# Moving the recurrence's sum and what follows it to later slots in a pipelined encoder layer

## The reference

```python
xn = rmsnorm(x, norm_pre_w)
na_q, na_k, na_v, na_z, hg_q, hg_ff, hg_fb, hg_i, hg_z, gate_pre = split(xn @ w_in)
o_a = neighbourhood_attention(na_q, na_k, na_v, rpb) * silu(na_z)       # 16 heads of 64
o_b = scan(hg_q, k_fwd, hg_i, log_f_fwd) + flip(scan(flip(...)))        # 8 heads of 128, both directions
o_b = rmsnorm(o_b, hg_norm_w) * silu(hg_z)                              # per head of 128 channels
g_a, g_b = split(sigmoid(gate_pre + b_gate))
y = g_a * (o_a @ w_branch[:1024]) + g_b * (o_b @ w_branch[1024:])
out = x + rmsnorm(y @ w_out, norm_post_w)
```

## Time and profile before

| | us |
|---|---|
| median of 3 runs | 835.32 |
| lowest, highest | 834.16, 838.45 |
| the profiled execution | 836.1 |
| its span, first to last instruction | 834.4 |
| mean granted clock of PE in it | 0.997 |
| PE busy | 820.7 (98%) |
| DVE busy | 632.1 (76%) |
| ACT busy | 413.7 (50%) |
| POOL busy | 40.2 (5%) |

### The profile page before, as it was taken

How to read it: one execution, slowest core, us unless ns; L and a number is a source line. 1 busy time by engine, 2 the same in 40 slices (tenths; PEclk the granted TensorE clock), 3 DMA queues, 4 the chain that set the end, 5 groups by cost and what they waited for, 6 DMA issues and landing times.

```text
span 834.4 us, 15319 instructions
## 1 busy us (share of the span) xinstructions
PE 820.7 (98%) x5582; PEld 703.8 (84%) x5582; DVE 632.1 (76%) x1053; ACT 413.7 (50%) x706; POOL 40.2 (5%) x48
## 2 busy tenths in 40 slices
PE   9999999999999999999999999999999999999996
PEld 8888788888888888888888888888888888878884
DVE  4777747888888888888888897897785778765443
ACT  5744445445445445445445435535545555544442
POOL 5000100000000000000100000100000000000002
PEclk9999999999999999999999999999999999999998
DMA  9755777676576676566667666666557767675522
GB/s 329 277 178 181 198 190 182 174 196 165 160 196 164 167 195 171 159 181 170 174 179 180 167 168 168 188 166 186 155 160 195 220 188 197 202 275 193 185 104 101
DMA packets 246729, 153.98 MB, mean 185 GB/s; under 512 B 15288, under 2 KB 228368, under 8 KB 246288
## 3 DMA queue, kind: packets, MB, share of 16 engines
q1 hardware_dynamic: 245664, 149.17, 63.0%
q10 hardware_dynamic: 1008, 3.98, 1.3%
HBM read 151.04 MB, written 2.10 MB: 184 GB/s over the span
## 4 chain that ended last, share of the span: by engine, by line
PE 92%; DVE 4%; ACT 1%; issue 1%; POOL 0%; DMA 0%; POOLq 0%; ACTq 0%
PE psum L1174 47%; PE psum L1176 23%; PE psum L1416 3%; PE psum L1418 3%; PE psum L1417 3%; DVE w_lo L711 2%; PE psum L1227 2%; PE psum L1229 2%; PE psum L1228 2%; PE psum L1278 1%; ACT w_hi L448 1%; PE psum L1266 1%; PE psum L1243 1%; PE psum L1313 1%; PE psum L1256 1%
## 5 line engine op out<-in xcount | busy, mean ns | idle before, releaser
L1174 PE MATMUL psum<-act_hl,w_hi 128*128 128x512 f32 x1408 | 501.6, 400 | 1.7 <-DVE hg L732 1.0
L1176 PE MATMUL psum<-act_hl,w_lo 128*128 128x256 f32 x1408 | 394.4, 280 | 0.0
L711 DVE TENSOR_TENSOR w_lo<-raw,w_hi 128x1024 fp32r<-128x1024 f32 x272 | 323.7, 1228 | 81.9 <-ACT w_hi L448 81.6
L1174 PEld LDWEIGHTS psum<-act_hl,w_hi 128*128 128x128 f32 x1408 | 264.3, 188 | 66.3 <-issue 2.3
L448 ACT ACTIVATE w_hi<-raw 128x1024 fp32r<-128x1024 f32 x272 | 273.7, 1053 | 39.5 <-PE psum L1418 25.8
L1176 PEld LDWEIGHTS psum<-act_hl,w_lo 128*128 128x128 f32 x1408 | 265.8, 189 | 0.0
L462 ACT ACTIVATE part<-psum 128x256 f32<-128x256 f32 x88 | 33.7, 383 | 214.8 <-PE psum L1176 214.8
L1174 PE MATMUL psum<-branch_hl,w_hi 128*128 128x512 f32 x256 | 88.9, 394 | 0.0
L1176 PE MATMUL psum<-branch_hl,w_lo 128*128 128x256 f32 x256 | 70.9, 277 | 0.0
L1174 PEld LDWEIGHTS psum<-branch_hl,w_hi 128*128 128x128 f32 x256 | 48.0, 188 | 11.1
L1227 PE MATMUL psum<-w_hi,branch_hl 128*128 128x512 f32 x128 | 50.3, 393 | 1.0 <-DVE w_lo L711 1.0
(11 more groups left out here) (137 smaller groups left out, 686.3 us busy)
## 6 DMA issues: line engine op xcount, KB each, us to landing
raw<-in_w_in SPq DMA_DIRECT2D x103, 1024.0 KB, 5.8
raw<-in_w_branch SPq DMA_DIRECT2D x16, 1024.0 KB, 6.0
raw<-in_w_out SPq DMA_DIRECT2D x16, 1024.0 KB, 5.0
bias_t<-in_na_rel_bias SPq DMA_DIRECT2D x32, 96.0 KB, 5.8
big<-in_x SPq DMA_DIRECT2D x4, 512.0 KB, 8.4
big<-in_x ACTq DMA_DIRECT2D x2, 1024.0 KB, 6.1
out<-big SPq DMA_DIRECT2D x5, 256.0 KB, 2.7
raw<-in_w_in SPq DMA_DIRECT2D x2, 512.0 KB, 6.5
```

Source lines behind the costliest of these rows:

```text
L711: nc.vector.tensor_tensor(w_lo[:, i, :], raw[:, r, 1024 * h:1024 * (h + 1)], w_hi[:, i, :].bitcast(F32), ALU.subtract).then_inc(lo_ready, 1)
L1174: nc.tensor.matmul(sums[h][:, :], w_hi[:, i, w], operand[:, k, :], start=first, stop=False, skip_group_check=True)
L1176: ins = nc.tensor.matmul(sums[h][:, 0:T], w_lo[:, i, w], operand[:, k, 0:T], start=False, stop=last, skip_group_check=True)
```

## The change

The sum moves on PE from slot 6 to slot 9, behind the early near session of the next group. What follows it becomes a third routine, `finish(g - 2, s)`, that runs in the group after that: squares and mean square in slot 0, scaling in slot 1, the turn on PE in slot 2 ahead of the late near session, the output product in slot 2, its rounding and subtraction in slot 3. The tanh of `hz` moves on ACT from slot 0 to slot 4 and the output gate on DVE from slot 8 to slot 5, both still one group behind. DVE's `take_nearest` gets a wait for the sum, which reads the same scores. POOL's loop runs the power of group g - 2 ahead of the mask's add of group g. The tail does the same steps for its two last groups.

POOL:

```diff
             mask_bias(0)
-            with loop(pool, 1, NG) as g:
+            mask_bias(1)
+            with loop(pool, 2, NG) as g:
+                power(g - 2)
                 mask_bias(g)
-                power(g - 1)
+            power(NG - 2)
             power(NG - 1)
```

ACT:

```diff
                 if s == 0:
-                    tanh_half((hth, hz), g - 1, NSLOT_HZ, hz_tanh)
                     act.wait_ge(oa_ready, g)
...
-                if s == 6:
-                    out_square(g - 1)
-                if s == 7:
-                    out_scale(g - 1)
-                if s == 9:
-                    hgrn_hi(g - 1)
+                if s == 4:
+                    wait(act, ob_ready, g - 1)
+                    tanh_half((hth, hz), g - 1, NSLOT_HZ, hz_tanh)
+
+            def finish(g, s):
+
+                if s == 0:
+                    out_square(g)
+                if s == 1:
+                    out_scale(g)
+                if s == 3:
+                    hgrn_hi(g)
```

DVE:

```diff
                 if s == 9:
+                    if not first:
+                        dve.wait_ge(hg_out, g)
                     take_nearest(g)
...
-                if s == 8:
-                    hgrn_out(g - 1)
-                if s == 9:
-                    hgrn_lo(g - 1)
+                if s == 5:
+                    output_gate(g - 1)
+
+            def finish(g, s):
+
+                if s == 0:
+                    mean_square(g)
+                if s == 2:
+                    hgrn_out(g)
+                if s == 3:
+                    hgrn_lo(g)
...
                     split_tile(*place(g0, p, s + 1)[0:2])
+                    if third:
+                        finish(g - 2, s)
                     if not first:
                         previous(g, s)
                     attention(g, s, first)
-                    if s == 6 and not first:
-                        mean_square(g - 1)
```

PE:

```diff
-                if s == 5:
-                    hgrn_sum(g - 1)
-                if s == 7:
-                    turn_out(g - 1)
+            def finish(g, s):
+                if s == 1:
+                    turn_out(g)
...
+                            if third:
+                                finish(g - 2, s - 1)
                             if not first:
                                 previous(g, s - 1)
                             attention(g, s - 1)
+                            if s == IN_SLOTS - 1 and not first:
+                                hgrn_sum(g - 1)
```

More of the change, by code:

```diff
@@ L535, in previous, with group @@
                     nc.scalar.activation(i_now[:, :], at(big, g * 3 + (I_HOME - 3)), ACT.Copy).then_inc(i_ready, 1)
-                if s == 6:
-                    out_square(g - 1)
-                if s == 7:
-                    out_scale(g - 1)
-                if s == 9:
-                    hgrn_hi(g - 1)
-            def group(g0, p, first):
+                if s == 4:
[8 more added lines that the diff above has]
+                    hgrn_hi(g)
+            def group(g0, p, first, third=False):
                 g = g0 + p
@@ L625, in _ @@
                 for p in range(2):
-                    group(g0, p, False)
+                    group(g0, p, False, True)
             for t in range(TAIL):
@@ L631, in _ @@
                 previous(NG, t)
+                finish(NG - 2, t)
+                if t == 6:
+                    out_square(NG - 1)
+                if t == 7:
+                    out_scale(NG - 1)
                 take_part(place(NG, 0, t)[0], t % 2)
@@ L903, in mean_square, with output_gate @@
                 nc.vector.tensor_scalar(hg_ms, hg_ss, 1.0 / P, EPS, ALU.mult, ALU.add).then_inc(ms_ready, 1)
+            def output_gate(g):
+                dve.wait_ge(hz_tanh, g + 1)
+                nc.vector.scalar_tensor_tensor(out=hth, in0=hth, scalar=1.0, in1=hz, op0=ALU.add,
+                                               op1=ALU.mult).then_inc(ob_step, 1)
             def hgrn_out(g):
[L907 to L912, removed]
+                dve.wait_ge(ob_step, g + 1)
                 dve.wait_ge(o_turned, g + 1)
@@ L1384, in _, with tail_between @@
                 for p in range(2):
-                    group(g0, p, False)
+                    group(g0, p, False, True)
+            def tail_between(t):
+                if t == 0:
+                    attention(NG - 1, IN_SLOTS - 1)
+                else:
+                    finish(NG - 2, t - 1)
+                    previous(NG, t - 1)
+                if t == 6:
+                    hgrn_sum(NG - 1)
             for t in range(TAIL):
@@ L1388, in _ @@
                 pe.wait_ge(tile_out, made(NG, t - 2))
-                project(n, r, [ps_proj[t % 2]] * 2, act_hl,
-                        lambda: previous(NG, t - 1) if t else attention(NG - 1, IN_SLOTS - 1))
-            previous(NG, TAIL - 1)
+                project(n, r, [ps_proj[t % 2]] * 2, act_hl, lambda: tail_between(t))
+            turn_out(NG - 1)
             def branch(n, r, j):
```

2 lines of the change are left out of this document (1 added, 1 removed).

## The result

| | kernel before | changed kernel |
|---|---|---|
| median of the runs | 836.0 us (6 runs, 834.16 to 838.45) | 844.06 us (6 runs, 840.66 to 850.14) |
| profiled execution, its span | 836.1, 834.4 | 844.07, 842.3 |
| busy on PE, DVE, POOL | 820.7, 632.1, 40.2 | 822.3, 629.9, 38.9 |

The change makes the kernel slower: ratio 1.0093, with a 95% interval of 1.0072 to 1.0115. The forecast was 842.5. Sign and size came out, but most of the sum did not: of 7.9 us of span only 2.3 lie at the wait on which the forecast put 6.9. The changed kernel's own runs also spread more than those of the kernel before, and their mean granted clock differs: 0.998 in the fastest (840.66), 0.989 in the slowest (850.14), 0.994 to 0.996 in the four between.

The account below looks back on a forecast made before the run. PE, busy 98%, bounds the kernel; its own terms were 0, waits 6.9 us: span 834.4 + 6.9 = 841.3, 843.0 as an execution, 842.2 on the median's footing, stated as 842.5, range 836.5 to 847.5.

Parts of the forecast that it names:

- the wait on which the forecast put 6.9: PE waiting at the late near session for DVE's level 6 products, 0.72 to 1.44 us in each of groups 2 to 7.
- PE's own terms: On PE, moving the sum costs 0; joining the output's turn to another interruption saves 0 to 0.6 us, taken as 0.
- The pace: Half tiles on PE run quick or slow, 0.05 us apart; moved interruptions shuffle this, taken as 0, range 2 down, 1.5 up.
- POOL's order: On POOL the mask's add follows the power at once, falls into DVE's slots 0 and 1 and holds DVE there, 2.07 lost.
- The size of D: Delay of DVE's level 6 products: 0.16 mean square, 0.2 power, 2.07 mask's add, 2.43 us in all.
- The power's 0.2: POOL's power slowing DVE's products in slot 0, taken as 0.2 us by overlap, between bounds of 0 and 0.69.
- the formula: PE's wait per group: delay of the level 6 products minus margin minus 0.22, less 0.30 in groups 4 and 6.
- The margins of groups 4 and 6: Time level 6 is ready before PE's late session asks: 1.19 and 1.18, plus a DVE gap of 0.30.
- (C): Rival: POOL's power also holds DVE for its whole 0.69, waits 9.8 us in all, 845.1; chance 0.13.
- (B): Rival: little or no change, mask's add holding DVE where it does not count, or pace giving 3 us back; chance 0.27.
- (D): Rival: faster, level 6 delay under 1.0, no stall, nearly all halves quick on PE, -4.2, 831; chance 0.04.
- The signs that I named: Right: add behind power, 2 us DVE product, PE idle 0.7 to 1.5 at late session; wrong: e.g. PE waiting for w_lo.

## Why the prediction was right, and where it was wrong

**PE's own terms: right.** The move of the sum and the turn costs nothing that can be seen in the pitch of the w_hi matmuls around their interruptions; the turn stands ahead of the late session at 300.98.

**The pace: inside its bounds.** 17 quick halves for 36, +0.95, with 1.5 up kept for it. It isn't a free term, though: of halves that stand ahead of a wait, a quick pace is given back at it.

**POOL's order: right in mechanism.** The add stands directly behind the power, one DVE product beside it takes 1.95, and the late session waits for the level 6 product. The add alone does this to the kernel before, and putting it first takes it away.

**The size of D: the step that failed.** I had 0.16 + 0.2 + 2.07 = 2.43; it was 0.07 + 0 + 1.53 = 1.60. Of the 0.83 too much, 0.54 is the hold. I took the 2.28 and the 0.63 behind it in the earlier trace rows as two slowed operations that "take 0.42" otherwise. But products of that level take 0.63 with nothing beside them. The kernel before in group 5, where the add lies over a split instead:

```profile
461.65 0.63 DVE L791 TENSOR_TENSOR hg<-hg 128x256 f32<-128x256 f32 x1
462.32 0.64 DVE L796 TENSOR_TENSOR hg<-hg 128x256 f32<-128x256 f32 x1
```

So the hold in the earlier trace rows was 2.28 - 0.63 = 1.65, the very number that the split gave, and which I kept only for the lower end. Beside the level 3 product it was a little less again, 1.53. The power's 0.2 was 0, and the mean square takes 0.07 of DVE's time to the next start, not its duration. With 1.60 the formula gives 1.60 - 0.87 - 0.22 = 0.51 in group 3, measured 0.55, and 2.1 over the four groups that waited, measured 2.3. The formula held, its input didn't. The wrong base by itself, 0.42 in each of six groups, is 2.5 of the 6.9.

**The margins of groups 4 and 6: half right.** They are wider by 0.3, as I had from the earlier trace rows, but I didn't ask why. Both follow a jump: PE had stood there and DVE had not. The margin moves with that stall; with a longer one the wait was 0, without one 1.07 and 0.40.

**What no step had: 4.5 us at the jumps**, 2.9 of idle time and 1.6 of clock. The forecast said that the move of the sum to slot 9 costs 0, by its length. It moved PE's last half tile against a load that another engine times, and so the fetch behind it. The longer gap then cost clock as well. The two errors, 4.6 too much at the late session and 4.5 too little at the jumps, are of opposite sign, and the forecast's closeness is that coincidence: the right time came out by luck.

**The rivals.** (C), the power holding DVE for its whole time, fell: with the power beside them the products kept 0.42, in the changed kernel and with the mask's add in front. The Trainium skill ("SBUF — State Buffer", section "Who interferes with whom") has the lock held for the full instruction. For the 128x768 add the trace agrees, 1.53 of its 1.84; for the power, 0.80 long, it does not: the product at 291.41 starts inside it and keeps its 0.42, and the measurement decides. It was the power that was longer there, 0.80 for the 0.69 of the earlier trace rows. (B), little or no change, needed D below 1.9, and D was 1.60; its mechanism, the add somewhere else, did not come, only its size: with the jumps quiet the change is at 839.31, where (B) had 838.8 for half the stall. The rest of the loss was the fetch. (D) had D wrong and the pace too.

**The signs that I named.** Of those for being right, four came: the order on POOL, the DVE product of about 2 us in slot 0, the late session released by level 6 (in four groups of six), and no long product in slot 7 of the looped groups. Its waits were 0.54 to 0.67, below the 0.7 to 1.5 that I gave, and PE's idle time rose by 5.2 in the loop (6.3 over the span) rather than 7, more than half of it at the jumps. One of the signs of being wrong came as well, PE waiting for a `w_lo`: it was the longest wait of all, and behind that name stood the fetch.

## What to carry to other kernels

Before a sum is made from an operation's slowed duration, look up the same shape in the same place undisturbed: one wrong base put 2.5 us too much into a term of 6.9 that measured 2.3. A move on the bounding engine also shifts everything that other engines time against it; list the loads in flight where that engine jumps, since here its next instructions came over the same DMA engines. And where a margin is wider after a loop's jump than elsewhere, ask whether it is borrowed from a stall: here part of it was, and went with it. Last, a forecast that lands near the measured time is not yet right; only the waits by place showed that two errors had met.

## What the runs showed of the hardware

**An instruction fetch can stand behind a weight load.** Around the jump of PE's loop a 16 KB packet on the instruction queue is needed; behind a 1 MB load it started 3.27 us after PE began its last half tile, and PE stood 3.25 us. Delaying that load by hand brought the start to -0.02 and the stalls of 3.25 and 1.37 to 0 and 0.17 (839.31 for 844.06, POOL's order unchanged, and in spite of more waits at the late session). In the loop of the kernel before this queue's packets are 11 to 22 us apart, except at the two jumps (and the loop's end), where a second follows the first within 3.8 us (346.99 and 350.76 at the first). The Trainium skill ("Runtime: NRT & Kernel Launch", section "Instruction fetch mechanics") says that instructions are refilled in blocks of 16 KiB, and that a taken branch to a target outside the current window of two pages forces a fetch before execution can go on; the packets here have that size, and the stalls stand at the jump. Which of the two packets the branch asks for no run shows; the first starts while PE is still in its last half tile. Why its start moves when instructions are added far ahead stays open: in the changed kernel 32 more took the first stall away and not the second, in the kernel before with its late load they moved the first packet from 0.63 to 1.22, and 12 fewer moved it hardly (0.65 to 0.64).

**The releaser in a trace can be wrong for it.** PE's 3.25 us are put down to `w_lo`, the 1.37 to `hg` and others to "issue", though all are the same jump.

**An idle stretch of 3.25 us was followed by 3.4 us at a granted clock of 0.51**, and one of 3.33 by 3.5 at 0.55; idle stretches of 0.99 and 1.37 at the jumps by none.

**POOL's add holds one DVE operation, not several**: 1.53, 1.64 and 1.65 in the changed kernel, in the one with the add alone in slot 0, and in the kernel before, and a 128x2 power beside such products holds none.

**The pace of the projection.** Halves run at about 0.347 or 0.353 us a pair of w_hi and w_lo, and switch at interruptions. The count of quick ones went from 17 to 52 over these kernels. What sets it stays open.
